# Gated linear attention: outputs with tokens on the partitions, state steps of 128 tokens, transposes back

## The reference

```
proj = h @ w_in;  q, k, v, r = split(proj)
glog = log_sigmoid((h @ w_g1) @ w_g2 + b_g) / 16
# per head, chunks of 64 tokens
b = cumsum(glog within the chunk);  b_last = b at its end;  b_ref = b at its middle
A = (q * exp(b - b_ref)) @ (k * exp(b_ref - b)).T, causal within the chunk
o_intra = A @ v
# from chunk to chunk
o_inter = (q * exp(b)) @ state
state   = exp(b_last) * state + (k * exp(b_last - b)).T @ v
o = rmsnorm(o_intra + o_inter, g_onorm) * silu(r);  mix = o @ w_out
```

## Time and profile before

| | |
|---|---|
| median of 3 runs | 2094.8 us (2092.53 to 2095.17) |
| the profiled execution | 2092.58 us, span 2090.8 us |
| granted TensorE clock, mean over the span | 0.987 |
| TensorE busy | 99% of the span |
| VectorE, ScalarE, GpSimd busy | 44%, 34%, 5% |
| transfers | 197.12 MB, 94 GB/s over the span |

### The profile page before, as it was taken

How to read it: one execution, slowest core, us unless ns; L and a number is a source line. 1 busy time by engine, 2 the same in 40 slices (tenths; PEclk the granted TensorE clock), 3 DMA queues, 4 the chain that set the end, 5 groups by cost and what they waited for, 6 DMA issues and landing times. The chain is left out here.

```text
span 2090.8 us, 24776 instructions
## 1 busy us (share of the span) xinstructions
PE 2066.3 (99%) x10008; PEld 1743.1 (83%) x10008; DVE 921.8 (44%) x1004; ACT 712.1 (34%) x846; POOL 98.7 (5%) x106
## 2 busy tenths in 40 slices
PE   8999999999999999999999999999999999999998
PEld 6888888799988888888888888888898888888887
DVE  4343333476555455333333434333366544333333
ACT  5222222354444444222222422232245433222212
POOL 1000001000001001000001000001002010000000
PEclk9999999998899999999999999999999999999999
DMA  4222223211133323333232332222243123332231
GB/s 162 98 85 98 95 96 106 87 61 51 51 101 101 100 95 108 100 100 100 92 99 90 101 100 86 94 95 96 96 134 123 41 81 101 100 100 91 89 107 56
DMA packets 192701, 197.12 MB, mean 94 GB/s; under 512 B 3554, under 2 KB 191072, under 8 KB 192640
## 3 DMA queue, kind: packets, MB, share of 16 engines
q1 hardware_dynamic: 191104, 192.95, 28.1%
q0 software_dynamic: 928, 2.25, 0.3%
q10 hardware_dynamic: 608, 1.06, 0.1%
HBM read 194.15 MB, written 2.10 MB: 94 GB/s over the span
## 5 line engine op out<-in xcount | busy, mean ns | idle before, releaser
L310 PE MATMUL ps<-h_hi,w_hi 128*128 128x512 f32 (+1 forms) x1728 | 670.9, 388 | 6.8 <-DVE w_lo L1456 5.1
L311 PE MATMUL ps<-h_lo,w_hi 128*128 128x512 f32 (+1 forms) x1728 | 667.0, 386 | 0.0
L312 PE MATMUL ps<-h_hi,w_lo 128*128 128x512 f32 (+1 forms) x1728 | 666.9, 386 | 0.0
L1456 DVE TENSOR_TENSOR w_lo<-raw,w_hi 128x2048 fp32r<-128x2048 f32 (+3 forms) x192 | 416.8, 2171 | 474.2 <-ACT w_hi L1012 474.2
L1012 ACT ACTIVATE w_hi<-raw 128x2048 fp32r<-128x2048 f32 (+3 forms) x192 | 346.9, 1807 | 263.7 <-PE ps L312 263.7
L310 PEld LDWEIGHTS ps<-h_hi,w_hi 128*128 128x128 f32 x1728 | 325.7, 188 | 75.4 <-issue 7.5
L312 PEld LDWEIGHTS ps<-h_hi,w_lo 128*128 128x128 f32 x1728 | 325.4, 188 | 65.5
L311 PEld LDWEIGHTS ps<-h_lo,w_hi 128*128 128x128 f32 x1728 | 325.7, 188 | 64.7 <-issue 0.7
L310 PE MATMUL ps<-mid_hi,w_hi 128*128 128x512 f32 x704 | 274.0, 389 | 0.0
L311 PE MATMUL ps<-mid_lo,w_hi 128*128 128x512 f32 x704 | 273.9, 389 | 0.0
L312 PE MATMUL ps<-mid_hi,w_lo 128*128 128x512 f32 x704 | 273.9, 389 | 0.0
(11 more groups left out here) (320 smaller groups left out, 1903.1 us busy)
## 6 DMA issues: line engine op xcount, KB each, us to landing
raw<-in_ffn_w_gu SPq DMA_DIRECT2D x87, 1024.0 KB, 5.0
raw<-in_ffn_w_down SPq DMA_DIRECT2D x32, 1024.0 KB, 5.1
raw<-in_x_w_kv SPq DMA_DIRECT2D x16, 1024.0 KB, 5.4
raw<-in_ffn_w_down SPq DMA_DIRECT2D x16, 768.0 KB, 4.3
raw<-in_gla_w_in SPq DMA_DIRECT2D x12, 1024.0 KB, 5.1
raw<-in_x_w_q SPq DMA_DIRECT2D x8, 1024.0 KB, 5.1
raw<-in_x_w_o SPq DMA_DIRECT2D x8, 1024.0 KB, 5.0
raw<-in_gla_w_out SPq DMA_DIRECT2D x8, 512.0 KB, 3.4
```

The lines of the kernel that those rows point to most:

```text
L310: nc.tensor.matmul(out_ap, left[0], right[0], start=first, stop=False)
L311: nc.tensor.matmul(out_ap, left[0], right[1], start=False, stop=False)
L312: return nc.tensor.matmul(out_ap, left[1], right[0], start=False, stop=last)
L1456: return nc.vector.tensor_tensor(out_ap, value, hi.bitcast(F32), ALU.subtract)
```

## The change

- Outputs are made with tokens on the partitions, 256 value channels streaming: for each tile of 128 tokens the masked scores are the weights and `v` streams, and `qin` is the weights and the state streams. 21 matmuls of 256 columns for a head.
- Chunks of 128 tokens: the running sum b goes over 128, the mask is the full triangle, there are 3 state steps, their updates with all 128 rows. The scores within each 64 tokens stay as they were. The block of the later 64 tokens against the earlier 64 of a tile has its own reference, b at the end of the first 64: `cross_qk`, a difference, two exponentials, two products, a split, and 12 matmuls of 64 columns a head, which overwrite this block.
- The norm: ScalarE squares four pieces of 256 with its accumulator summing over the channels, which are now in the free dimension, and takes the root; VectorE takes the reciprocal and scales on the way out of PSUM into `o_tok`. `gla_norm`, `spread_norm`, `value_root`, `value_inverse` and `value_scale` go.
- `gla_transpose`: 8 transposes a head bring `o_tok` back to channels on the partitions (places `t0` to `t3`), where VectorE multiplies by gain and gate (`gated`).

```diff
-    GLA_ORDER = ("Q0", "K0", "V0", "R0", "V1", "R1", "c0", "Q1", "K1", "V2", "c1", "R2", "V3", ("OUT", 0, 0), "c2",
-                 ("OUT", 0, 1), ("OUT", 0, 2), ("OUT", 0, 3), "R3", "c3")
+    GLA_ORDER = ("Q0", "K0", "V0", "R0", "V1", "R1", "c0", "Q1", "t0", "K1", "V2", "c1", "R2", "t1", "V3", ("OUT", 0, 0),
+                 "c2", ("OUT", 0, 1), ("OUT", 0, 2), "t2", ("OUT", 0, 3), "R3", "c3")
...
     def place_cross_keys(i):
         for pair in range(4):
             place(("xk", i, pair), 2, 2, C)
+            if (i, pair) == (0, 1):
+                place("t3", 2, 2)
...
             def gla_scores(h):
...
+                pe.wait_ge(sig.cross_lo_ready, h + 1)
+                for tt in range(T):
+                    ks, qs = slice(tt * P, tt * P + CH), slice(tt * P + CH, (tt + 1) * P)
+                    last = three_products(ps[0:CH, 5, qs], (cross_hi[:, ks], cross_lo[:, ks]),
+                                          (cross_hi[:, qs], cross_lo[:, qs]), True, True)
...
             def gla_updates(h):
...
+                if h > 0:
+                    pe.wait_ge(sig.s_ready, 3 * h)
+                for tt in range(T - 1):
+                    three_products(ps[:, 6 + tt // 2, (tt % 2) * DV:(tt % 2 + 1) * DV], (kst_hi[:, tt, :], kst_lo[:, tt, :]),
+                                   (v_hi[:, h % 2, tt, :], v_lo[:, h % 2, tt, :]), True, True).then_inc(sig.kv_done, 1)
...
             def gla_outputs(h):
...
+                    for tt in (2 * c, 2 * c + 1):
+                        vs = slice((tt % 2) * DV, (tt % 2 + 1) * DV)
+                        last = three_products(ps[:, bank, vs], (am_hi[:, tt, :], am_lo[:, tt, :]),
+                                              (v_hi[:, h % 2, tt, :], v_lo[:, h % 2, tt, :]), True, tt == 0)
+                        if tt > 0:
+                            ts = slice(tt * P, (tt + 1) * P)
+                            pe.wait_ge(sig.s_lo_ready, 3 * h + tt)
+                            last = three_products(ps[:, bank, vs], (qin_hi[:, ts], qin_lo[:, ts]),
+                                                  (S_hi[:, tt - 1, :], S_lo[:, tt - 1, :]), False, True)
+                    last.then_inc(sig.part_done, 1)
+
+            def gla_transpose(h):
+
+                pe.wait_ge(sig.evacuated, at[f"c{h}"].out + 2)
+                for c in range(2):
+                    bank = chunk_bank(at[f"t{h}"].out + c)
                     for tt in range(T):
...
+                        last = nc.tensor.transpose(ps[:, bank, tt * P:(tt + 1) * P], o_tok[:, tt, c * P:(c + 1) * P],
+                                                   ident[:])
                     last.then_inc(sig.part_done, 1)
...
-            project("Q1", hh, middle=lambda: gla_norm(0))
-            spread_norm(0)
+            project("Q1", hh)
+            gla_transpose(0)
             project("K1", hh, middle=lambda: gla_updates(1))
...
-            cross_keys(0, (0,))
-            gla_norm(3)
-            cross_keys(0, (1, 2))
-            spread_norm(3)
-            cross_keys(0, (3,))
+            cross_keys(0, (0, 1))
+            gla_transpose(3)
+            cross_keys(0, (2, 3))
...
                 nc.scalar.activation(e[:, 0, :], e[:, 0, :], ACT.Exp, scale=1.0 / TAU).then_inc(sig.exp_ready, 1)
+                act.wait_ge(sig.cross_diff, h + 1)
+                for half, sign in ((0, -1.0), (1, 1.0)):
+                    nc.scalar.activation(halves(cross_qk[:])[:, :, half, :], halves(cross_qk[:])[:, :, half, :], ACT.Exp,
+                                         scale=sign / TAU).then_inc(sig.cross_exp, 1)
...
             def outputs(h):
...
+                for tt in range(T):
+                    bank = part(f"c{h}", tt // 2)
+                    nc.scalar.activation(sq[:].rearrange("p a (b n) -> p (a b) n", n=DV)[:, tt, :],
+                                         ps[:, bank, (tt % 2) * DV:(tt % 2 + 1) * DV], ACT.Square,
+                                         scale=float(DV) ** -0.5, accum_out=o_rms[:, tt:tt + 1])\
+                      .then_inc(sig.o_squared, 1)
+                act.wait_ge(sig.o_squared, T * (h + 1))
+                nc.scalar.activation(o_rms[:], o_rms[:], ACT.Sqrt, bias=eps[:]).then_inc(sig.o_root, 1)
...
             def decayed_qk(h, meanwhile=None):
...
+                nc.vector.tensor_tensor(by_chunk(cross_qk[:], P), bt, bt[:, :, CH - 1:CH].broadcast_to([P, T, P]),
+                                        ALU.subtract).then_inc(sig.cross_diff, 1)
...
+                dve.wait_ge(sig.cross_exp, 2 * h + 2)
+                for half, factor in ((0, k), (1, q)):
+                    nc.vector.tensor_tensor(halves(cross_qk[:])[:, :, half, :], halves(factor[:, h % 2, :])[:, :, half, :],
+                                            halves(cross_qk[:])[:, :, half, :], ALU.mult).then_inc(sig.cross_scaled, 1)
...
+                lo_part(cross_lo[:], cross_qk[:], cross_hi[:]).then_inc(sig.cross_lo_ready, 1)
...
             def outputs(h):
 
+                dve.wait_ge(sig.o_root, h + 1)
+                nc.vector.reciprocal(o_rms[:], o_rms[:]).then_inc(sig.o_rms, 1)
+                dve.wait_ge(sig.o_rms, h + 1)
                 if h > 0:
                     dve.wait_ge(sig.o_lo_ready, h)
+                for tt in range(T):
+                    bank = part(f"c{h}", tt // 2)
+                    done = nc.vector.tensor_scalar_mul(o_tok[:, tt, :], ps[:, bank, (tt % 2) * DV:(tt % 2 + 1) * DV],
+                                                       o_rms[:, tt:tt + 1])
+                    if tt % 2 == 1:
+                        done.then_inc(sig.evacuated, 1)
+
+            def gated(h):
+
+                dve.wait_ge(sig.part_done, at[f"t{h}"].part + 2)
```

More of the change, by code:

```diff
@@ L382, in _ @@
                     load_fixed(name, io.gla_w_out[0], 0, 4, name[2] * COLS)
-                elif name[0] != "c":
+                elif name[0] not in "ct":
                     first = {"Q": 0, "K": D // 2, "V": D, "R": 2 * D}[name[0]]
@@ L711, in gla_outputs @@
                     bank = chunk_bank(at[f"c{h}"].out + c)
-                    vs = slice(c * P, (c + 1) * P)
-                    for tt in range(T):
[L714 to L723, removed]
@@ L724, in gla_outputs @@
-                    last.then_inc(sig.part_done, 1)
[L726 to L745, removed]
+                    for tt in (2 * c, 2 * c + 1):
[7 more added lines that the diff above has]
+                                                  (S_hi[:, tt - 1, :], S_lo[:, tt - 1, :]), False, True)
@@ L942, in _ @@
             gla_scores(2)
[L943 to L944 removed]
+            project("R2", hh)
+            gla_transpose(1)
             project_rows("V3", hh, T, middle=lambda: gla_updates(2))
@@ L1136, in states @@
             def states(h):
-                for n in range(NCH - 1):
-                    act.wait_ge(sig.s_ready, 7 * h + n + 1)
+                for n in range(T - 1):
+                    act.wait_ge(sig.s_ready, 3 * h + n + 1)
                     hi_part(S_hi[:, n, :], S[:, n % 2, :]).then_inc(sig.s_hi_ready, 1)
@@ L1156, in outputs @@
             def outputs(h):
-                for c in range(2):
-                    bank = part(f"c{h}", c)
-                    nc.scalar.activation(sq[:, c, :], ps[:, bank, :], ACT.Square).then_inc(sig.o_squared, 1)
-            def value_root(h):
-                act.wait_ge(sig.o_summed, h + 1)
-                nc.scalar.activation(o_rms[:], ps[:, 7, 0:T], ACT.Sqrt, bias=eps[:]).then_inc(sig.o_root, 1)
+                for tt in range(T):
[6 more added lines that the diff above has]
+                nc.scalar.activation(o_rms[:], o_rms[:], ACT.Sqrt, bias=eps[:]).then_inc(sig.o_root, 1)
             def value_split(h):
-                act.wait_ge(sig.o_scaled, 2 * h + 2)
+                act.wait_ge(sig.evacuated, at[f"t{h}"].out + 2)
                 hi_part(o_hi[:, 2 * (h % 2):2 * (h % 2) + 2, :], u[:]).then_inc(sig.o_hi_ready, 1)
@@ L1657, in output_gate @@
                 if h >= 2:
-                    dve.wait_ge(sig.evacuated, at[f"c{h - 2}"].out + 2)
+                    dve.wait_ge(sig.evacuated, at[f"t{h - 2}"].out + 2)
                 for c in range(2):
@@ L1675, in outputs @@
                                                    ALU.mult, ALU.mult).then_inc(sig.evacuated, 1)
-            def value_inverse(h):
-                dve.wait_ge(sig.o_root, h + 1)
-                nc.vector.reciprocal(o_rms[:], o_rms[:]).then_inc(sig.o_rms, 1)
-            def value_scale(h):
-                dve.wait_ge(sig.evacuated, at[f"c{h}"].out + 2)
-                dve.wait_ge(sig.o_spread, h + 1)
-                for c in range(2):
-                    nc.vector.tensor_tensor(u[:, c, :], u[:, c, :], ps[:, 7, :], ALU.mult).then_inc(sig.o_scaled, 1)
             def value_split(h):
-                dve.wait_ge(sig.o_scaled, 2 * h + 2)
+                dve.wait_ge(sig.evacuated, at[f"t{h}"].out + 2)
                 dve.wait_ge(sig.o_hi_ready, h + 1)
@@ L1954, in _ @@
             scores_split(1)
```

(16 more changed lines are left out.)

99 lines of the change are left out of this document (43 added, 56 removed).

## The result

The changed kernel took 2073.1 us (median of four runs, 2072.2 to 2075.7) against 2095.0 for the kernel before in the same comparison: a ratio of 0.990, interval 0.9883 to 0.9917. Forecast were 2056 us, range 2048 to 2068. The sign was right; the time lies 5 us above the range. The profiled execution has a span of 2071.6 us and took 2073.3.

A forecast was written before the change was run, and what follows sets the result against it. TensorE, busy 99% of the span, was taken as the bound: -43.4 us of its work plus 5.9 given back made -37.5, from 2092.6 to 2055.1, stated as 2056 us, range 2048 to 2068.

The forecast's parts named there:

- rivals A to F: A as summed 0.57; B VectorE/ScalarE bound 0.20; C clock falls 0.15; D slower 0.03; E no change 0.02; F better 0.03.
- Outputs: Four output stages on TensorE: 66 matmuls each become 21 of 256 columns, 38.81 to 10.08 us, minus 28.7.
- Half clock behind the outputs: Scores and Q1's first half, or their like, behind each output stage: back at full clock, 9.7 us less.
- Cross scores: 12 new matmuls a head on TensorE, 64 weight columns and 64 streamed: 0.09 us each, 4.4 us more.
- Waits: TensorE waiting at scores(0) 0.4, OUT 1 2.2, first cross key 3.3 with pacing; none at K1, V3: 5.9 us given back.
- rival C: Gated-attention stage: the clock still falls, two to four times at 1.3 to 3.8 us each, 2058 to 2070 us; chance 0.15.
- pacing: First cross-key pass: eight m_lo at 0.40 us pace steps that need 0.36, 0.3 us more.
- norm sums: Norm sums on TensorE, 1.71 us each, four times, are gone: minus 6.8 us.
- updates: State updates on TensorE: 21 half-height matmuls a head become nine of full height, minus 2.6 us.
- eight transposes: Per head on TensorE, eight 128x128 transposes at 0.83 us replace the spread's four fp32 matmuls, priced the same: zero.
- rival D: Slower: TensorE at 1.2 GHz through the stage, some 171 us at full clock; 2112 us at three times the extra; chance 0.03.
- Table loads: ScalarE's table load priced at 1.28 us; by the skill's 2.66, K1 waits about 2.3 and time is some 5 us longer.

The follow-up runs named there:

- experiments 1 and 9: Changed kernel with phase region 128 numbers wide instead of 120: 2056.7 us; changed kernel with unused mean_dv allocated again: 2058.1 us.
- experiments 7 and 8: Kernel before, h and w 32 bytes higher: 2110.0 us; changed kernel, h, w and mid all 32 bytes above a multiple of 128: 2057.4 us.
- experiment 12: Changed kernel with phase region 128 wide, head 3's memory(0) before R's split, OUT's first residual earlier, everything 384 bytes higher: 2050.2 us.

## Why the prediction was wrong, point by point

**The step that failed** is one sentence: "Nothing outside the stage changes; the weights' transfers have the same order, and they keep up as long as their splits do." I had looked for what the other stages wait for and who issues their transfers, not at where their operands lie. The removed `mean_dv` moved them, and 16.4 us came back on it (experiments 1 and 9). With that step mended the kernel takes 2056.7 us, where 2056 was forecast. None of the rivals A to F had this: all of them place their loss or gain inside the stage, which was 36.7 us shorter.

**Outputs**: foretold 10.08 us for four, measured 10.59 busy, so -28.2 for -28.7, at 119 to 120 ns each and clock 1.00. Right.

**Half clock behind the outputs**: it went as told; the only slow stretches left stand behind two waits, below. The term was a little small: in head 3 the 4.41 us of the earlier trace rows held 21 matmuls, not 24, so the excess was 1.9 and not 1.5, and the four together 10.1 and not 9.7.

**Cross scores**: mis-sized. I took 0.09 us each between 0 and 0.108. The row of head 1's:

```profile
470.80 0.22 PE L315 MATMUL ps<-cross_hi 128*64 128x64 f32 x1
470.86 0.22 PE L316 MATMUL ps<-cross_lo,cross_hi 128*64 128x64 f32 x1
470.92 0.22 PE L317 MATMUL ps<-cross_hi,cross_lo 128*64 128x64 f32 x1
```

They start 0.06 us apart, 0.67 for twelve (470.66 to 471.33), 2.7 for four heads in place of 4.4. The half-height row (0.077) was nearer than the pace of the scores.

**Waits**: x 2.4 (foretold 2.2), m_lo 3.3 (3.0), scores(0) 0.26 (0.4), none at K1 or V3, as told. Not foretold: 0.57 for k in front of scores(1) and 0.2 for v_lo.

**The clock behind the waits** is where rival C was right and the forecast, which argued from 1.6 us at 669.22, was not. Behind the wait for x:

```profile
546.68 0.47 PE L315 MATMUL ps<-o_hi,w_hi 128*128 128x512 f32 x1 [2.37 <-DVE x L1540]
546.99 0.40 PE L316 MATMUL ps<-o_lo,w_hi 128*128 128x512 f32 x1
...
548.18 0.63 PE L315 MATMUL ps<-o_hi,w_hi 128*128 128x512 f32 x1
548.60 0.63 PE L316 MATMUL ps<-o_lo,w_hi 128*128 128x512 f32 x1
549.03 0.63 PE L317 MATMUL ps<-o_hi,w_lo 128*128 128x512 f32 x1
```

Six matmuls at full pace, then 0.43 us from start to start: the half clock came 1.5 us after the wait had ended. The 24 took 7.20 us in place of 5.5 (24 x 0.229): 1.7 lost. Behind m_lo the clock fell 1.0 us after the wait had ended, and 37 matmuls took 5.98 us (588.06 to 594.04) in place of 4.4 (37 x 0.120), 1.5 more. All of it is the half clock (16 matmuls 0.21 us apart, 589.10 to 592.50); of the 0.3 foretold as pacing next to nothing shows. Whether the clock falls behind such a wait differs from profile to profile; the last section has the count.

**The sum of the stage**: -28.2 - 10.1 - 6.8 (norm sums) - 2.6 (updates) - 0.3 (eight transposes took 0.79 us a head, the spread 0.81 and once 0.98) + 2.7 (cross scores) + 6.4 (waits; the one of scores(0) ends where the stage is counted from) + 3.2 (clock) = -35.7, against 36.7 measured. 1.0 us remains unplaced. The errors of single terms nearly cancelled, and the agreement of 37.5 with 36.7 is in part luck. (In rival D the stage at full clock is given as 171 us; 210.7 less 37.5 is 173.)

**Table loads**: the Trainium skill, page "ScalarE: Activation LUTs", section "What ACT_TABLE_LOAD costs", would have K1 wait. It did not, and no drain shows: in the changed kernel ScalarE's last read ended at 547.61, 0.01 us ahead of the load. ScalarE there, root and exponential each behind a load:

```profile
547.62 1.28 ACT L1154 ACT_TABLE_LOAD   x1
548.92 0.30 ACT L1154 ACTIVATE o_rms<-o_rms,eps 128x4 f32<-128x4 f32 x1
549.23 1.28 ACT L1118 ACT_TABLE_LOAD   x1
550.53 0.63 ACT L1118 ACTIVATE e<-b 128x512 f32<-128x512 f32 x1
```

1.30 us from load to the next activation, twice in a row; the row decides against 2.66 here.

**Open**: why the distance between the two operands matters, and why matmuls of 512 and of 256 columns answer to it in opposite ways. That it is this distance is shown by the placements of the table; the mechanism in the chip is not. Only steps of 32 bytes were tried.

## What to carry to other kernels

When an edit adds or drops any buffer, however small, compare the addresses of all streamed operands and weights before and after, and keep those that a hot 512-column matmul reads together at equal phase against 128 bytes; if a total does not add up, look at the groups that nobody edited, by pace and not by waits. And price a wait of TensorE of over 2 us at more than its own length: here 2.4 cost 1.7 more behind it, while waits of 1.8 and less cost only themselves. That price is a chance and not a certainty, and what falls in one execution need not fall in the next.

## What was not expected of the hardware

- A 512-column matmul takes 226.7 to 227.1 ns from start to start when streamed operand and weights start at the same byte modulo 128, 228.9 when they are 64 apart, 233.3 to 233.7 when they are 32 or 96 apart. Their own alignment doesn't matter (experiments 7 and 8), and 512 bytes bring no more than 128 (experiment 12). A 256-column matmul takes 119.8 ns at equal phase and 116.7 to 118.3 when they are apart. The Trainium skill, page "SBUF — State Buffer", section "Operand start alignment", asks only for a start at a multiple of the element size and says that this is about legality, not speed; all places here satisfy it.
- In the changed kernel the clock fell to 1.2 GHz 1.4 us after the wait of 2.4 had ended and 1.0 us after the one of 3.3, when dense matmuls were running again. In the profiles of all 14 kernels together it fell during, or within 1.5 us behind, 6 of 6 waits of 3.2 to 3.4 us, 22 of 35 waits of 2.3 to 2.7, 4 of 20 of 1.9 to 2.1, and none of 25 of 1.3 to 1.8. The same wait of 2.5 for p_tok, in layer 1, had a fall in 7 of the 14 profiles and none in the other 7.
- Matmuls with 64 weight columns and 64 streamed follow each other after 0.056 us (0.67 / 12), half the 0.110 of narrow ones with 128 weight columns.
